# The causal mask of two attentions, added by an accumulating transpose in place of a product

## Chip, core and metric

The kernel runs on one core of a Trainium2 chip. The metric is the device time of one execution in microseconds, as the median of several runs; lower is better.

## The reference

A decoder trunk of two layers over 512 rows of 1024 values, all f32. In each layer a normalised input goes through one projection; four mixers read its columns: a block attention A (4 heads of 64), an RWKV-7 recurrence B, a gated unit C and a differential attention D (4 heads, two maps of 32 each). Their outputs go through one output projection, are added to the input, and a mixture of 32 experts follows (top 1 of 4 groups, top 2 of its 8 experts). What the change touches is the mask of A and D:

```
s = einsum(q, k) * scale
mask = arange(end)[None, :] <= (q0 + arange(128))[:, None]
p = softmax(where(mask, s, -inf))
```

With 512 rows and blocks of 256, attention A is plain causal attention too.

## The kernel before

All engines are programmed by hand and meet at semaphores. In each layer TensorE turns the normalised rows, projects them (L572, L583), and then runs the mixers by one written-out order, `mixer_steps`: steps of the recurrence (P products, T turns, V solve, L levels of the block inverse, Z/B/S chunks, F finish), each followed by some units of attention. Every engine walks the same order, so each has a fixed queue.

An attention unit is one tile of 128 queries (i = 0 to 3) and one head: 16 units for A and 16 for D in each layer. D has two maps in each unit, A one, so there are 48 maps a layer and 96 in all. A map's scores lie in PSUM bank 5 or 6. In `attn(m, u)` TensorE writes the scores of unit u (L754), adds the mask to the last 128 columns (L757), turns the probabilities of unit u-1 (L764, into bank 7) and multiplies those of unit u-2 with the values (L776). VectorE takes the row maximum (L1469) once the mask is in, ScalarE the exponential with its sum (L1138), VectorE the reciprocal and, for D, the difference of the two maps (L1457 to L1462); ScalarE copies the turned probabilities (L1146). The scores of a map wait until the exponential of the map that held the bank is done; L764 waits for the exponential (A) or for L1462 (D).

The constants come in one table, CF: `ident` (identity), `causal` (0 where the key is not after the query, -1e30 elsewhere), `unit` (four 128x128 masks of 0 and 1 for the recurrence; the second is 1 where the partition is not after the column), `head`, `ones` and others. Products with no use for their result (L623, `keep_busy`) stand between some steps of the recurrence that belongs to D.

The recurrence of D needs inverted blocks: VectorE solves them (L1403 to L1406), and SyncE's queue takes them through HBM (L433 to L442) before L663 and L680 read them. The same queue loads the experts' weights in tiles of 2 MB (`fill`, L453 and L455); the first tile is asked for early, the next ones after `mixed_done` (DVE L1494), `mt_ps` and the residual sums (L1587), and the others as tiles come free. A further pass for an expert with over 64 tokens runs only if there is one.

Of the kernel before, what the change touches and what calls it, by code (L numbers as in the profile page):

```python
# [10 lines left out]
ALU = mybir.AluOpType  # L11
# [3 lines left out]
P = 128  # L15
# [22 lines left out]
NEG = -1.0e30  # L38
# [31 lines left out]
def layout(fields):  # L70
    at, out = 0, {}
    for name, n in fields:
        out[name] = (at, n)
        at += n
    return out, at
# [3 lines left out]
CF, NCF = layout([("ident", P), ("causal", P), ("unit", 4 * P), ("head", P), ("ones", P),  # L79
                  ("cosA", NT * 8), ("sinA", NT * 8), ("cosD", NT * 4), ("sinD", NT * 4),  # L80
                  ("down4", GROUPS), ("down8", EPG), ("slot0", NE), ("hop", NE), ("blocks", NOV)])
# [8 lines left out]
def build(nc, x, w_in, w_out, pcol, prow, w2a2, g2, sguT, router, norm2_g, w_gate, w_up, w_down,  # L90
          final_g, cf, cm, out):
    ctx = ExitStack()
    with ctx:
        def sb(name, n, dt=F32):
            return ctx.enter_context(nc.sbuf_tensor(name, [P, n], dt))
# [13 lines left out]
        def at(layer, s, n):  # L109

            return s, layer * adds[s.num] + n
# [13 lines left out]
        CFs = sb("CF", NCF)  # L125
# [13 lines left out]
        PS = [PSALL[:, i * BN:(i + 1) * BN] for i in range(8)]  # L139

        def cst(name):
            lo, n = CF[name]
            return CFs[:, lo:lo + n]
# [236 lines left out]
        for p in range(10):  # L380
            adds[tile_full[p].num] = 16 * (tile_base[p] + sum(at == p for at, _, _ in PLACE))
# [4 lines left out]
        with nc.Block() as block:  # L386
# [155 lines left out]
            def _(pe):  # L542
                mm, tr = nc.tensor.matmul, nc.tensor.transpose
                ident = cst("ident")
                pe.wait_ge(ident_in, 16)

                for layer in range(DEPTH):
# [182 lines left out]
                    def attn(m, u):  # L730
                        s, nm = mix[m], 2 if m == "D" else 1
# [11 lines left out]
                        if u < 16:  # L743
                            i, h = unit_of[u]
                            w = (i + 1) * P
                            for a in range(nm):
                                n = u if m == "A" else 2 * u + a
                                if n >= 2:
                                    pe.wait_ge(*at(layer, s["exped"], n - 1))
                                if m == "A":  # L750
                                    rows = slice((h % 2) * 64, (h % 2) * 64 + 64)
                                else:
                                    rows = slice((h % 2) * 64 + a * 32, (h % 2) * 64 + a * 32 + 32)
                                mm(PS[5 + n % 2][:, 0:w], QKT[rows, h // 2, i * P:w], QKT[rows, 2 + h // 2, 0:w], start=True, stop=False)  # L754
                            for a in range(nm):
                                n = u if m == "A" else 2 * u + a
                                mm(PS[5 + n % 2][:, i * P:w], ident, cst("causal"), start=False, stop=True).then_inc(s["scores"], 1)  # L757
                        if 1 <= u <= 16:
                            i, h = unit_of[u - 1]
                            pe.wait_ge(*at(layer, s["exped"] if m == "A" else s["probs"], u))  # L760
# [5 lines left out]
                        if u >= 2:  # L766
                            n = u - 2
                            i, h = unit_of[n]
# [6 lines left out]
                            for b in range(i + 1):  # L775
                                last = mm(PS[0][:, 0:HD], PT[:, n % 2, b * P:(b + 1) * P], VAD[:, b, v0:v0 + HD],  # L776
                                          start=(b == 0), stop=(b == i))
                            last.then_inc(s["o_ps"], 1)

                    run_mixers(proj=project, rwkv=rwkv, attn=attn, sgu_out=mix_positions)  # L780


# [30 lines left out]
                    for n, ks in ((0, (0, 1, 4, 5)), (0, (2, 3, 6, 7)), (1, range(KD))):  # L813
# [10 lines left out]
                        w = SLOT[n].rearrange("p (k n) -> p k n", k=KD)  # L824
# [170 lines left out]
                    for i in range(NT):  # L995
                        for n in range(2):
                            part = slice(n * CAP, (n + 1) * CAP)
                            mm(PS[2 * i + n][:, :], SHARE_T[part, i * P:(i + 1) * P], YS[0][part, :],
                               start=True, stop=True).then_inc(y2_ps, 1)
# [198 lines left out]
            def _(dve):  # L1198
                V = nc.vector
# [53 lines left out]
                for layer in range(DEPTH):  # L1253
# [19 lines left out]
                    if layer == 0:  # L1273
                        dve.wait_ge(const_in, 33)
                        V.tensor_copy(CMs[:, :], SLOT[5][:, 0:2 * ON_PE * P])
                        ones = CFs[:, CF["ones"][0]:CF["ones"][0] + CAP]
                        V.tensor_tensor_scan(IOTA[:, :], ones, ones, -1.0, ALU.mult, ALU.add)
                        V.tensor_reduce(lane, CFs[:, CF["unit"][0] + P:CF["unit"][0] + 2 * P], AX.X, ALU.add).then_inc(row_named, 1)
                        dve.wait_ge(row_named, 1)
                        V.tensor_scalar(lane, lane, -1.0, float(P), ALU.mult, ALU.add).then_inc(row_named, 1)  # L1280
                        dve.wait_ge(row_named, 2)
                        V.tensor_scalar(upper, lane, float(CAP) - 0.5, None, ALU.is_ge).then_inc(row_named, 1)
                        V.tensor_scalar(TOKEN[:, :, 0], CFs[:, CF["slot0"][0]:CF["slot0"][0] + 2 * NT:2], lane, -NOWHERE, ALU.add, ALU.add)
                        V.tensor_scalar(TAG[:, :, 0], CFs[:, CF["slot0"][0]:CF["slot0"][0] + 16:2], lane, None, ALU.add).then_inc(row_named, 1)
# [294 lines left out]
                    for g in range(8):  # L1579
                        n, i = divmod(g, 4)  # L1580
# [46 lines left out]
                    for half in range(2):  # L1627
                        s = slice(half * HALF, (half + 1) * HALF)
# [156 lines left out]
                    with dve.If(nov > 0):  # L1785
                        with dve.Fori(0, nov) as j:
# [17 lines left out]
                            for r in range(8):  # L1804
                                i, n = divmod(r, 2)
# [206 lines left out]
```

## Time and profile before

| | |
|---|---|
| median of 3 runs | 1883.64 us (1880.81 to 1886.59) |
| profiled execution | 1870.49 us, span 1868.6 us |
| granted TensorE clock, mean | 0.976 |
| TensorE matrix instructions | 1636.9 us busy, x9360 |
| L757, the mask | x192, 40.3 us busy |
| attention units, layer 0 | from 228 to 365 us |
| attention units, layer 1 | from 1150 to 1286 us |

The rows are those of one profiled execution; the span is from its first instruction to its last. Times on the chain of work that ended last count what each step adds to it. The busy time of matrix instructions overlaps from one to the next, since they are pipelined; the distance of their starts is what one costs in a row of them. A granted clock of 1.00 is 2.4 GHz, 0.50 is 1.2 GHz.

### The profile page before, as it was taken

How to read it: one execution, taken by the hardware profiler on the slowest of the kernel's cores; microseconds unless marked ns; L12 is line 12 of the kernel's file. 1: busy time of each engine (PE TensorE's matmuls, PEld its weight loads, DVE VectorE, ACT ScalarE, POOL GpSimd, SP SyncE). 2: the span in 40 equal slices, each digit the busy share in tenths (PEclk: the TensorE clock that was granted, in tenths of full speed). 3: DMA queues.
4: the chain of work that ended last, by engine and by line, in shares of the span. 5: the costliest groups of instructions: out<-in, count | busy, mean ns of one | idle time of the engine just before them, and what ended most of it. 6: DMA issues, size and time to landing. Idle time of an engine off the chain costs nothing.

```text
span 1868.6 us, 22709 instructions
## 1 busy us (share of the span) xinstructions
PE 1636.9 (88%) x9360; PEld 996.0 (53%) x9360; DVE 622.8 (33%) x1419; ACT 278.0 (15%) x638; POOL 158.0 (8%) x175
## 2 busy tenths in 40 slices
PE   7999899999899889777699999899997998888773
PEld 4445567547566555444344456675574665554441
DVE  2174175626212111221322632656251211112115
ACT  3121243401000000000123112332100000000001
POOL 0010000000311111110000101000021111111000
PEclk9999999998999999999999999999998999999997
DMA  9212001056999999999922120011589999999995
GB/s 315 90 45 99 1 4 52 1 247 255 414 424 424 422 425 424 422 423 421 373 75 90 43 96 1 14 41 50 214 362 421 424 424 424 423 424 423 423 421 207
DMA packets 71945, 480.31 MB, mean 257 GB/s; under 512 B 25181, under 2 KB 27165, under 8 KB 37024
## 3 DMA queue, kind: packets, MB, share of 16 engines
q1 hardware_dynamic: 61472, 462.52, 60.2%
q0 software_dynamic: 10368, 16.30, 2.4%
q8 instruction: 77, 1.26, 0.3%
q14 instruction: 28, 0.23, 0.0%
HBM read 468.05 MB, written 28.11 MB: 266 GB/s over the span
## 4 chain that ended last, share of the span: by engine, by line
PE 59%; DMA 27%; DVE 7%; issue 3%; ACT 2%; SPq 1%; POOL 1%; DVEq 0%; POOLq 0%; ACTq 0%
PE banks L583 11%; PE banks L877 11%; PE banks L830 6%; DMA TOK<-in_w_up 6%; PE banks L572 6%; PE banks L892 5%; DMA RING<-in_w_up 5%; DMA RING<-in_w_gate 5%; DMA TOK<-in_w_gate 5%; DMA RING<-in_w_down 2%; PE banks L754 2%; PE banks L855 2%; PE banks L776 1%; PE banks L663 1%; PE banks L757 1%
## 5 line engine op out<-in xcount | busy, mean ns | idle before, releaser
L877 PE MATMUL banks<-RING,XS 128*64 128x256 f32 x2752 | 319.4, 388 | 47.7 <-DMA RING<-in_w_up 28.6
L877 PEld LDWEIGHTS banks<-RING,XS 128*64 128x64 f32 x2752 | 222.4, 140 | 155.3 <-issue 42.8
L583 PE MATMUL banks<-RING,XNT 128*128 128x512 f32 x512 | 224.2, 595 | 0.1
L892 PE MATMUL banks<-RING,XS 128*64 128x512 f32 x768 | 177.4, 602 | 28.3 <-issue 15.2
L1711 DVE SCALAR_TENSOR_TENSOR XS<-banks,TABLE,XS 128x256 f32<-128x256 f32 x58 | 28.1, 484 | 433.3 <-PE banks L877 433.3
L583 PEld LDWEIGHTS banks<-RING,XNT 128*128 128x128 f32 x512 | 96.8, 191 | 117.7 <-issue 116.7
L1177 ACT ACTIVATE XS<-banks,TABLE 128x256 f32<-128x256 f32 x58 | 27.4, 473 | 797.1 <-PE banks L877 797.1
L892 PEld LDWEIGHTS banks<-RING,XS 128*64 128x64 f32 x768 | 60.9, 138 | 112.1 <-issue 112.1
L1753 DVE COPY XS<-banks 128x512 f32<-128x512 f32 x64 | 44.2, 691 | 218.2 <-PE banks L892 191.3
L1923 POOL DMA_INDIRECT y_rows<-XS,SOLVE x64 | 66.2, 1034 | 531.5 <-DVE XS L1753 513.1
L572 PE MATMUL banks<-XNT,RING 128*128 128x512 f32 x256 | 110.2, 592 | 0.0
L877 PE MATMUL banks<-TOK,XS 128*64 128x256 f32 x832 | 94.4, 380 | 14.0 <-DMA TOK<-in_w_gate 7.2
L877 PEld LDWEIGHTS banks<-TOK,XS 128*64 128x64 f32 x832 | 67.9, 137 | 44.0 <-issue 12.7
L830 PE MATMUL banks<-RING,XNT 128*128 128x512 f32 x192 | 86.5, 595 | 1.7 <-ACT XNT L1151 1.7
L572 PEld LDWEIGHTS banks<-XNT,RING 128*128 128x128 f32 x256 | 48.6, 190 | 61.2 <-issue 61.2
L1138 ACT ACTIVATE XNT<-banks,SMALL 128x128 f32<-128x128 f32 (+3 forms) x96 | 50.1, 525 | 129.4 <-DVE SMALL L1469 115.7
L830 PEld LDWEIGHTS banks<-RING,XNT 128*128 128x128 f32 x192 | 35.5, 190 | 42.3 <-issue 40.2
L1469 DVE TENSOR_REDUCE SMALL<-banks 128x1 f32<-128x128 f32 (+3 forms) x96 | 44.5, 488 | 37.7 <-PE banks L757 36.5
L754 PE MATMUL banks<-XNT 32*128 32x128 f32 (+7 forms) x192 | 53.0, 483 | 4.5 <-ACT XNT L1128 2.7
L870 PE MATMUL banks<-CF,XS 128*128 128x128 f32 x256 | 38.7, 296 | 15.9 <-DMA XS<-x_rows,SOLVE 15.9
L1891 POOL DMA_INDIRECT XS<-x_rows,SOLVE x32 | 33.8, 1057 | 190.9 <-PE banks L870 188.6
L883 PE MATMUL banks<-CF,XS 128*128 128x128 f32 x132 | 30.5, 313 | 20.9 <-DVE XS L1711 18.4
(334 smaller groups left out, 1892.2 us busy)
## 6 DMA issues: line engine op xcount, KB each, us to landing
RING<-in_w_down SPq DMA_DIRECT2D x46, 2048.0 KB, 27.1
RING<-in_w_up SPq DMA_DIRECT2D x44, 2048.0 KB, 27.2
RING<-in_w_gate SPq DMA_DIRECT2D x42, 2048.0 KB, 26.3
RING<-in_w_in_blocks SPq DMA_DIRECT2D x12, 2048.0 KB, 9.7
TOK<-in_w_gate SPq DMA_DIRECT2D x12, 2048.0 KB, 32.2
TOK<-in_w_up SPq DMA_DIRECT2D x10, 2048.0 KB, 32.4
XNT<-in_w_down SPq DMA_DIRECT2D x8, 2048.0 KB, 31.1
TOK<-in_w_down SPq DMA_DIRECT2D x6, 2048.0 KB, 24.0
```

The costliest lines, as they stand in the source:

```text
L572: last = mm(bank[:, :], w[:, k, j * P:(j + 1) * P], XNT[:, k, :], start=(k == 0), stop=(k == KD - 1))
L583: last = mm(bank[:, :], XNT[:, k, i * P:(i + 1) * P], w[:, k, :], start=(k == 0), stop=(k == KD - 1))
L754: mm(PS[5 + n % 2][:, 0:w], QKT[rows, h // 2, i * P:w], QKT[rows, 2 + h // 2, 0:w], start=True, stop=False)
L830: last = mm(PS[4 * n + i][:, :], src[:, i * P:(i + 1) * P], w[:, k, :], start=(k == 0), stop=(k == KD - 1))
L855: last = mm(PS[k // 4][:, (k % 4) * P:(k % 4 + 1) * P], X3[:, i, :].rearrange("t (p k) -> t p k", k=KD)[:, :, k], HOT[:, i, :], start=(i = ...
L870: last = tr(PS[k // 4][:, (k % 4) * P:(k % 4) * P + n], rows[:, :, k], ident[0:n, 0:n])
L877: last = mm(bank[f * CAP:(f + 1) * CAP, 0:256], rows[:, k, :], w[:, k, f * 256:(f + 1) * 256], start=(k == 0), stop=(k == KD - 1))
L892: last = mm(PS[5][n * CAP:(n + 1) * CAP, :], HT[:, j, f * CAP:(f + 1) * CAP], w[:, k, n * BN:(n + 1) * BN], start=(k == 0), stop=(k == KF ...
L1138: ac(PB[:, u % 2, a, 0:w], PS[5 + n % 2][:, 0:w], ACT.Exp, bias=nmx[:, col:col + 1], accum_out=sums[:, col:col + 1]).then_inc(s["exped"], 1)
L1469: V.tensor_reduce(nmx[:, base + n:base + n + 1], PS[5 + n % 2][:, 0:w], AX.X, ALU.max, negate=True).then_inc(s["maxed"], 1)
L1753: V.tensor_copy(YS[h], PS[5][:, :]).then_inc(y2_copied, 1)
L1923: pool.indirect_dma_start(y_halves, bass.IndirectOffsetOnAxis(ap=YROW[:, e:e + 1], axis=0), YS[h], None, bounds_check=4 * SEQ - 1, oob_is_ ...
```

## The change

The mask is no longer the moving operand of a product with the identity. Its transpose is the stationary operand of a matrix instruction in transpose mode, with the identity moving, that adds to the bank (`start=False`). The output is (maskT)T, the same mask. For this the `causal` place of CF has to hold the transposed mask; VectorE writes it once, in layer 0, as (unit - 1) * 1e30 from the second mask of `unit`. The mask that comes with CF is overwritten by it and no longer read.

```diff
@@ TensorE, attn(m, u)
                             for a in range(nm):
                                 n = u if m == "A" else 2 * u + a
-                                mm(PS[5 + n % 2][:, i * P:w], ident, cst("causal"), start=False, stop=True).then_inc(s["scores"], 1)
+                                mm(PS[5 + n % 2][:, i * P:w], cst("causal"), ident, start=False, stop=True, is_transpose=True).then_inc(s["scores"], 1)
@@ VectorE, layer 0
                         V.tensor_tensor_scan(IOTA[:, :], ones, ones, -1.0, ALU.mult, ALU.add)
+                        V.tensor_scalar(cst("causal"), CFs[:, CF["unit"][0] + P:CF["unit"][0] + 2 * P], 1.0, -NEG, ALU.subtract, ALU.mult)
                         V.tensor_reduce(lane, CFs[:, CF["unit"][0] + P:CF["unit"][0] + 2 * P], AX.X, ALU.add).then_inc(row_named, 1)
```

## Rows read from the trace of the kernel before

**Rows 1.** The page: busy time by engine, and the chain that ended last.
```profile
PE 1636.9 (88%) x9360; PEld 996.0 (53%) x9360; DVE 622.8 (33%) x1419; ACT 278.0 (15%) x638; POOL 158.0 (8%) x175
...
PE 59%; DMA 27%; DVE 7%; issue 3%; ACT 2%; SPq 1%; POOL 1%; DVEq 0%; POOLq 0%; ACTq 0%
```

**Rows 2.** Windows: us; PE, PEld, DVE, ACT, POOL busy; clock, DMA share, GB/s.
```profile
600.00:900.00 300.00, 248.48 (x1804) 148.80 (x1801) 52.02 (x82) 9.94 (x21) 35.89 (x32) 0.99 1.01 423
```

**Rows 3.** Waits of the DMA queue of SyncE: us in total, times, longest.
```profile
SPq L453 <- DVEq L1494: 174.5, 2, 87.3
...
SPq L492 <- DVE X L1587: 94.8, 8, 21.6
```

**Rows 4.** Instructions of L757 and of L764: duration in ns, min/median/max.
```profile
L757 PE MATMUL banks<-CF x192: 275/275/582, 228.6 to 1274.7; 128*128 128x128 f32 x192
...
L764 PE MATMUL banks<-CF,XNT x160: 272/273/421, 230.1 to 1278.7; 128*128 128x128 f32 x160
```

**Rows 5.** Timeline of TensorE around a pair and a single mask: start, us, what.
```profile
1261.22 0.71 PE L757 MATMUL banks<-CF 128*128 128x128 f32 x4
1261.77 0.49 PE L764 MATMUL banks<-CF,XNT 128*128 128x128 f32 x3
1262.10 0.67 PE L776 MATMUL banks<-TOK,RING 128*128 128x64 f32 x5
...
228.16 0.48 PE L754 MATMUL banks<-XNT 64*128 64x128 f32 x2 [0.69 <-ACT XNT L1128]
228.57 0.49 PE L757 MATMUL banks<-CF 128*128 128x128 f32 x2
```

**Rows 6.** The chain in layer 0: masks, first and last, and two pairs.
```profile
228.64 0.42 PE banks L757 x2
...
290.24 1.15 PE banks L757 x4
...
317.70 0.64 PE banks L757 x4
...
352.49 0.43 PE banks L757 x2
```

**Rows 7.** Windows of layer 0's attention stretches, columns as in rows 2.
```profile
226.00:230.00 4.00, 3.06 (x20) 2.37 (x20) 0.67 (x3) 3.59 (x7) 0.00 (x0) 1.00 0.00 0
...
281.00:285.00 4.00, 3.06 (x26) 2.52 (x26) 0.28 (x1) 2.17 (x4) 0.00 (x0) 1.00 0.18 37
...
288.00:294.00 6.00, 5.77 (x26) 5.14 (x26) 2.24 (x8) 2.27 (x11) 0.00 (x0) 0.50 0.39 92
...
316.00:352.00 36.00, 35.29 (x238) 24.38 (x237) 24.62 (x66) 17.11 (x57) 0.00 (x0) 1.00 0.00 1
```

**Rows 8.** Waits from 225 to 366 us: us in total, times, longest.
```profile
PE banks L764 <- DVE XNT L1462: 2.9, 6, 1.0
PE banks L764 <- ACT RING L1146: 2.8, 4, 1.0
...
DVE SMALL L1469 <- PE banks L757: 18.1, 17, 4.9
```

**Rows 9.** SyncE's queue at the second attention's start, and KB and us to landing.
```profile
287.25 4.09 SPq L442 DMA_DIRECT2D RING<-inv_e  x8
...
RING<-inv_e SPq DMA_DIRECT2D x32, 8.0 KB, 1.7
```

**Rows 10.** The chain behind those blocks, and the same products later.
```profile
291.93 3.16 PE banks L663 x16
295.09 0.89 PE banks L680 x8
...
300.99 1.84 PE banks L663 x16
```

**Rows 11.** Timeline of VectorE where the change adds its instruction.
```profile
24.61 0.26 DVE L1278 TENSOR_REDUCE SMALL<-CF 128x1 f32<-128x128 f32 x1
...
30.45 0.69 DVE L1287 TENSOR_TENSOR RING<-RING,CF 128x512 f32<-128x512 f32 x1 [4.93 <-DMA SMALL<-in_norm_g]
```

## The prediction

> **What bounds the kernel now.** I read the page first: TensorE is busy for 88% of the span and is 59% of the chain that ended last; DMA is 27% of that chain [rows 1]. The windows tell where each rules. From 600 to 900 us (the experts) the 16 DMA engines are full at 423 GB/s and TensorE is busy for 248 of 300 us [rows 2]: time saved on TensorE there would be lost to the weights. The masks are not there. They are 192 instructions of L757, in two stretches of some 137 us, one a layer, where the attention units run between the steps of the RWKV part and DMA is nearly idle. What I must know is whether an earlier end of that stretch reaches the end of the kernel. The waits of the DMA queue answer it: the queue stood 174.5 us in all for DVEq L1494 (mixed_done) and 94.8 us for L1587 (residual sums) [rows 3]. So all expert weights but the first tile are asked for only behind the mixers, and the full DMA stretch keeps its length and only begins earlier. I carry a microsecond saved in the mixers to the end at full value, in each layer.
>
> **What one mask costs, and what its turn will cost.** The mask of a map is one product of 128x128 f32, and the trace has two MATMUL for it, each with its weight load: x192 for 96 maps (275 ns each at the median) [rows 4]. The transpose of L764 is of the same size, is also f32, and has one instruction for each 128x128 (x160 for 160 blocks), of 273 ns. A duration holds the way through the array, so the price is the spacing: four mask instructions start at 1261.22 and the first transpose at 1261.77, which is 0.55 us for five slots (one is the first weight load), and three transposes take 1261.77 to 1262.10, 0.33 us [rows 5]. Both kinds take 0.11 us a slot. The turn thus takes one slot in place of two: 0.11 us saved a map, at the full clock. All 96 maps would give 10.6 us.
>
> **What of it lies on the path.** The chain of layer 0 passes 14 times through a single map (L757 x2) and 8 times through a pair (x4), from 228.64 to 352.49 us [rows 6]; layer 1 has the same counts. That is 14 + 16 = 30 of 48 maps a layer; the other 18 lie beside the L1416 merges, beside the L1387 products, or beside a wait for L1462, and save nothing. 60 x 0.11 = 6.6 us. Three maps of each layer, the pair at 290.24 and the map before it, run at half clock, where a pair takes 1.15 us on the chain against 0.64 [rows 6], so each saves another 0.11: 0.7 us in both layers. The upper bound is 7.3 us.
>
> The lower bound takes only the pairs, where TensorE is busy 35.3 of 36.0 us (316 to 352) [rows 7]: 32 x 0.11 = 3.5 us. The single maps of the first attention share their place with waits for the exponents, and TensorE's own waits in layer 0 are 2.9 us for L1462 and 2.8 us for L1146 [rows 8]; a shorter mask also brings these forward, since the maximum (L1469) waits for it, 18.1 us in 17 cases. So I take three of four parts of the bound and a little: 5.7 us. One cover has to hold: the inverted blocks come by DMA at the start of the second attention. Their last issue ends at 291.34 and lands 1.7 us later, at 293.0 [rows 9], and the first product that reads them (L680) starts at 295.09 [rows 10]. Some 2 us of cover stand against at most 13 maps since 262 us and their half-clock extra, 1.8 us, and the solve moves up itself. No wait should appear.
>
> **The other parts.** The stationary operand is now the mask and the moving one the identity: no instruction more. One VectorE instruction is added, in layer 0 only, which makes the mask on the chip from the `unit` table. The reduction of the same 128x128 at 24.61 takes 0.26 us, and behind this run VectorE idles 4.93 us until L1287 at 30.45 [rows 11]. Price 0 to 0.3 us, I take 0: that wait hides it, and without the cover it would be 0.3 us once. Semaphores and DMAs are as before. The form itself, a transpose that adds to a bank, is not in this trace. Its cost lies between one slot (0.11, as L764) and two (0.22, as the product); it is nearest to L764, so one. There is one more unknown: the first mask starts 0.41 us behind a product of two slots (228.16 to 228.57) [rows 5], so 0.2 us pass when the 64-row operands give way to 128 rows. Both forms have that change, so I count nothing for it.
>
> Sum: 1868.6 - 5.7 = 1862.9 us of span, 1864.8 for the profiled execution (1870.49 before). The median of the runs shown is 13.1 us above that execution; the saving is taken off it: 1883.6 - 5.7 = 1878 us, 0.30% less.
>
> **The rivals.**
> *Nothing gained (the adding form takes two slots, or a wait absorbs each slot).* For it: no row shows the form, and waits for VectorE are close in the pairs. Against it: product to transpose and transpose to product follow at 0.11 us in [rows 5]. Time 1884.
> *The clock, on the other side.* Before, the granted clock fell from 1.00 (2.4 GHz) to 0.50 (1.2 GHz) for 288 to 294 us, after a stretch with idle time on TensorE [rows 7]. What this costs: 16 products of L663 take 3.16 us there and 1.84 later [rows 10], and with L754 and the masks the chain loses some 2.3 us. The change takes work out of just such thin stretches (226 to 230 is busy 3.06 of 4.00 us and still has 1.00). One more fall a layer costs 4.6 us and leaves 1883 (no change). The sign turns at 3 falls more in both layers together, and it is slower by over 0.3% from 5. If the stretch of the pairs (36 us, nearly all TensorE) lost the clock as well, up to 30 us a layer would be added: 1938. Against it: from 281 to 285, where 16 transposes of L740 are most of the work, the clock stayed at 1.00 [rows 7].
> The Trainium skill (TensorE: Matmul & The Clock Gate, PE-mode transpose) says that a transpose doesn't count as busy for the clock as a product does. By that rule the masks would fall out of the activity wholly and the clock rival would be likely; by the row of 281 to 285 they lose half of it at most. The trace speaks against the rule, so I leave that rival small.
> *The mask does not add but overwrites.* Then the change doesn't do what it says: the diagonal blocks hold no scores, the router sees other rows, and an expert with over 64 tokens would bring an overflow pass with three loads of 2 MB, 15 us at 423 GB/s: 1893 or more.
> The Trainium skill (PSUM — Partial Sum Buffer, The four PSUM rules) says that an f32 transpose shares the marks by which a bank adds; no row here shows it.
> *More gained.* If the half-clock fall of each layer went away, another 4.6 us would go: 1873.
>
> **How the numbers follow.** The forecast, 3.5 to 7.3 us, has 0.74; nothing gained 0.12; one or two falls more 0.05; many falls 0.04; overwritten 0.02; more gained 0.03. 0.3% is 5.65 us, about what a measurement here can tell from no change, and it lies on my sum: of the 0.74, 0.42 is beyond it and 0.32 short of it. Faster 0.42 + 0.03 = 0.45; same 0.32 + 0.12 + 0.05 = 0.49, taken as 0.48; slower 0.07. The three runs before spread over 5.8 us, which I add half to either side: from 7.3 saved (1876.3) less 2.8 = 1873.5 to nothing gained (1883.6) and 1.9 of the spread, 1885.5.
>
> **What would show it.** L757 with 96 matrix instructions of about 273 ns and 96 weight loads; a pair on the chain at 0.42 us in place of 0.64; the stretch from the first L754 of a layer to its first L830 shorter by 2 to 3.6 us, and the end of each expert stretch earlier by the same; a clock of 0.50 in one stretch of some 7 us a layer. I am wrong if L757 still takes two slots, if L764 or L680 waits longer by what the masks gave, or if the clock row has more falls.

## The result and the profile after

| | before | after |
|---|---|---|
| median of 5 runs each | 1883.75 us (1880.81 to 1886.59) | 1872.61 us (1868.28 to 1874.56) |
| profiled execution | 1870.49 us, span 1868.6 | 1868.28 us, span 1866.4 |
| granted clock of it, mean | 0.976 | 0.975 |

The ratio is 0.9939 (95% interval 0.9921 to 0.9957): 11.1 us faster. Predicted were 5.7 us and 1878.0; the time lies 0.9 us below the range. Two numbers of this table already disagree: the medians differ by 11.1 us, the two profiled executions by 2.2. The profiled execution after is the fastest of its five; the one before is none of its five and lies 10 us under the lowest of them. Executions that took over 1.5% longer than the others of their kernel (four of 101 of the kernel before, 1909 to 3300 us, and one of a variant, 5798 us) are left out of all figures. The profile says which stretches got shorter, and by how much.

**The instruction.** The instructions of L757 in the trace after (columns as in [rows 4]):

```profile
L757 PEld LDWEIGHTS banks<-CF x96: 137/138/224, 228.1 to 1271.1; 128*128 128x128 f32 x96
L757 PE MATMUL banks<-CF x96: 272/328/474, 228.1 to 1271.2; 128*128 128x128 f32 x96
```

The weight loads of the same line in the trace before:

```profile
L757 PEld LDWEIGHTS banks<-CF x192: 186/189/333, 228.6 to 1274.6; 128*128 128x128 f32 x192
```

There are 96 where [rows 4] have 192, with 96 weight loads. The median of 328 ns in place of 275 is no higher price: the ends of matrix instructions are modelled, so the starts tell the price. The timeline of TensorE after, around the same pair as in [rows 5] and around the first single mask:

```profile
1271.08 0.44 PE L757 MATMUL banks<-CF 128*128 128x128 f32 x2
1271.35 0.60 PE L764 MATMUL banks<-CF,XNT 128*128 128x128 f32 x4
...
227.65 0.48 PE L754 MATMUL banks<-XNT 64*128 64x128 f32 x2 [0.69 <-ACT XNT L1128]
228.06 0.33 PE L757 MATMUL banks<-CF 128*128 128x128 f32 x1
228.23 0.56 PE L701 MATMUL banks<-RING 128*128 128x64 f32 x4
```

The product behind that single mask stood here in the trace before:

```profile
228.90 0.56 PE L701 MATMUL banks<-RING 128*128 128x64 f32 x4
```

From the pair to the transposes behind it pass 0.27 us where 0.55 passed [rows 5], which is 0.14 a map. From the single mask to L701 pass 0.17 us where 0.33 passed (228.57 to 228.90), which is 0.16 a map. Both are more than the slot of 0.11. In a row each form follows at 0.11 us, but the first instruction of a mask holds up the next one longer: by 0.21 us as a product and by 0.165 as a transpose (medians of the distances of starts). The median of the weight load fell as well, from 189 to 138 ns; that it sets this distance is likely, but not shown. By the distances of starts a layer frees 16 x 0.16 for A and 16 x 0.275 for the pairs of D, some 7.0 us at full clock, not the 5.3 of 48 x 0.11. The single mask still starts 0.41 us behind its L754 product, as before.

**The chain.** Layer 0 of the chain that ended last, after: some of the single masks, the pair at half clock with the products behind it, and the first and the last of seven pairs at full clock.

```profile
228.13 0.26 PE banks L757
...
229.20 0.26 PE banks L757
...
231.62 0.26 PE banks L757
...
237.19 0.27 PE banks L757
...
283.93 0.27 PE banks L757
...
288.17 0.62 PE banks L757 x2
...
289.32 3.52 PE banks L663 x16
292.85 1.40 PE banks L680 x8
...
315.97 0.37 PE banks L757 x2
...
349.45 0.37 PE banks L757 x2
```

Against [rows 6]: 0.37 us for a pair where 0.64 stood (predicted 0.42), 0.62 for the half-clock pair where 1.15 stood, 0.26 for a single one where 0.42 stood. Counted over the whole layer, the chain passes 12 single masks and 8 pairs, 28 maps, where it passed 30. Its time in L757 fell from 11.7 to 6.3 us, by 5.4. The stretch got shorter by only 2.7: the other half came back on other steps of the same chain. Steps of VectorE and ScalarE (L1462 and its neighbours, L1138, L1431, L1436) take 2.5 us more of it, L764 and L776 1.8, and L663 and L680 0.9; L754, the row maximum and issue take 2.6 less.

**Who waits.** Waits from 225 to 366 us, after (columns as in [rows 8]; the added VectorE line moves L1462 to L1463 and L1469 to L1470):

```profile
DVE SMALL L1470 <- PE banks L757: 14.6, 14, 4.7
...
PE banks L764 <- DVE XNT L1463: 4.6, 7, 1.1
...
PE banks L764 <- ACT RING L1146: 3.4, 4, 1.2
```

TensorE's two waits were 2.9 and 2.8 us [rows 8]; they are 4.6 and 3.4. So 2.3 us of what was freed in this layer came again as waits. VectorE's wait for the mask fell from 18.1 to 14.6 us.

**The stretch.** The marks that I compare all executions by are the first L740 and the first L830 of a layer, that is from the first transpose of the attention's Q and K to the first product behind the mixers. Timeline of TensorE in layer 0, before:

```profile
225.04 1.04 PE L740 MATMUL banks<-CF,TOK 128*128 128x128 f32 x8
...
367.42 1.13 PE L830 MATMUL banks<-RING,XNT 128*128 128x512 f32 x2 [0.85 <-ACT XNT L1151]
```

The same after, in layer 0 and then in layer 1:

```profile
224.53 1.04 PE L740 MATMUL banks<-CF,TOK 128*128 128x128 f32 x8
...
364.22 4.13 PE L830 MATMUL banks<-RING,XNT 128*128 128x512 f32 x9 [0.84 <-ACT XNT L1151]
...
1146.34 1.04 PE L740 MATMUL banks<-CF,TOK 128*128 128x128 f32 x8
...
1285.91 0.70 PE L830 MATMUL banks<-RING,XNT 128*128 128x512 f32 x1 [0.84 <-ACT XNT L1151]
```

142.38 us became 139.69 in layer 0 and 142.35 became 139.57 in layer 1: 2.69 + 2.78 = 5.5 us. The forecast for both was 5.7.

**The covers and the rest.** Windows after (columns as in [rows 2]), over the places of [rows 7] and [rows 2], each moved with its work:

```profile
225.00:229.00 4.00, 3.06 (x23) 2.33 (x20) 0.47 (x2) 3.55 (x7) 0.00 (x0) 1.00 0.00 0
280.00:284.00 4.00, 3.06 (x26) 2.39 (x26) 0.28 (x1) 2.17 (x4) 0.00 (x0) 1.00 0.18 38
287.00:294.00 7.00, 6.97 (x33) 6.75 (x34) 1.58 (x6) 2.66 (x10) 0.00 (x0) 0.52 0.45 115
315.00:350.00 35.00, 33.52 (x222) 22.08 (x221) 24.47 (x66) 16.35 (x53) 0.00 (x0) 1.00 0.00 1
600.00:900.00 300.00, 244.96 (x1752) 143.51 (x1750) 52.88 (x83) 9.47 (x20) 34.92 (x31) 0.98 1.01 423
```

The clock is as in [rows 7]: 1.00 in the thin stretches and in that of the pairs, one fall to half where the second attention starts. In the pairs' stretch TensorE is busy for 33.5 of 35 us where it was busy for 35.3 of 36 [rows 7]: it has slack now. The experts still fill the DMA engines at 423 GB/s. The added VectorE instruction and the next one on its engine, timeline after:

```profile
24.09 0.20 DVE L1278 TENSOR_SCALAR CF<-CF 128x128 f32<-128x128 f32 x1
...
29.81 0.69 DVE L1288 TENSOR_TENSOR RING<-RING,CF 128x512 f32<-128x512 f32 x1 [4.68 <-DMA SMALL<-in_norm_g]
```

0.20 us, with a wait for DMA of 4.68 us behind it (4.93 before [rows 11]): hidden.

**The way to the end.** The first loads of the expert weights behind the mixers start 3.2 us earlier in layer 0 (0.5 of it was there at the first L740, ahead of every mask), and the loads at the end of that layer's experts 3.8 us earlier. So nothing of the gain is lost in the DMA stretch. Then it shrinks to 0.5 us between 1087 us and the first L740 of layer 1, at 1146.34 (1146.87 before): in this execution the granted clock fell once more at 1119.8 us, for 6.8 us, where the execution before kept 1.00. Nothing that the change touches lies there. Of the 5.5 us gone from the two attention stretches the two profiled spans show 2.2.

### The profile page after: what moved, and what is told of

Same layout as the page of the kernel before. It is cut to its first block, busy times and chain, and to the rows that moved or that the text cites. A ratio compares the mean times of both kernels' runs of the same rounds, so it can differ in the third digit from the quotient of the medians.

```text
span 1866.4 us, 22518 instructions
## 1 busy us (share of the span) xinstructions
PE 1631.3 (87%) x9264; PEld 980.3 (53%) x9264; DVE 622.5 (33%) x1420; ACT 277.8 (15%) x638; POOL 158.7 (9%) x175
## 4 chain that ended last, share of the span: by engine, by line
PE 61%; DMA 23%; DVE 7%; SPq 4%; issue 3%; ACT 2%; another core or an unknown queue 1%; DVEq 0%; POOLq 0%; ACTq 0%
PE banks L877 12%; PE banks L583 12%; PE banks L892 7%; PE banks L830 6%; PE banks L572 6%; DMA TOK<-in_w_up 6%; DMA RING<-in_w_up 5%; DMA RING<-in_w_gate 3%; DMA RING<-in_w_down 2%; DMA TOK<-in_w_gate 2%; SPq L453 2%; DMA SCAN<-in_w_up 2%; PE banks L855 2%; PE banks L754 2%; PE banks L776 1%
## 5 line engine op out<-in xcount | busy, mean ns | idle before, releaser
L877 PE MATMUL banks<-RING,XS 128*64 128x256 f32 x2752 | 318.1, 387 | 53.2 <-DMA RING<-in_w_up 30.0
L877 PEld LDWEIGHTS banks<-RING,XS 128*64 128x64 f32 x2752 | 220.5, 139 | 162.6 <-issue 43.0
L877 PE MATMUL banks<-TOK,XS 128*64 128x256 f32 x832 | 94.4, 380 | 13.9 <-DMA TOK<-in_w_gate 8.1
L877 PEld LDWEIGHTS banks<-TOK,XS 128*64 128x64 f32 x832 | 67.4, 137 | 44.8 <-issue 11.7
L830 PE MATMUL banks<-RING,XNT 128*128 128x512 f32 x192 | 86.5, 595 | 1.7 <-ACT XNT L1151 1.7
L1138 ACT ACTIVATE XNT<-banks,SMALL 128x128 f32<-128x128 f32 (+3 forms) x96 | 50.1, 525 | 123.4 <-DVE SMALL L1470 106.8
L830 PEld LDWEIGHTS banks<-RING,XNT 128*128 128x128 f32 x192 | 35.5, 190 | 42.3 <-issue 40.2
L754 PE MATMUL banks<-XNT 32*128 32x128 f32 (+7 forms) x192 | 53.2, 483 | 5.1 <-ACT XNT L1128 2.7
L883 PE MATMUL banks<-CF,XS 128*128 128x128 f32 x132 | 30.5, 314 | 27.2 <-DVE XS L1712 18.4
L1470 DVE TENSOR_REDUCE SMALL<-banks 128x1 f32<-128x128 f32 (+3 forms) x96 | 44.1, 488 | 30.3 <-PE banks L757 29.4
L1417 DVE COPY_PREDICATED RING<-CM,banks 128x512 f32<-128x512 uint8 x40 | 29.2, 730 | 57.9 <-PE banks L682 30.3
```

What stands on the lines that cost most here:

```text
L830: last = mm(PS[4 * n + i][:, :], src[:, i * P:(i + 1) * P], w[:, k, :], start=(k == 0), stop=(k == KD - 1))
L877: last = mm(bank[f * CAP:(f + 1) * CAP, 0:256], rows[:, k, :], w[:, k, f * 256:(f + 1) * 256], start=(k == 0), stop=(k == KD - 1))
L1138: ac(PB[:, u % 2, a, 0:w], PS[5 + n % 2][:, 0:w], ACT.Exp, bias=nmx[:, col:col + 1], accum_out=sums[:, col:col + 1]).then_inc(s["exped"], 1)
L1470: V.tensor_reduce(nmx[:, base + n:base + n + 1], PS[5 + n % 2][:, 0:w], AX.X, ALU.max, negate=True).then_inc(s["maxed"], 1)
```

## The experiments

All ran in three sets; a set ran on one chip with the kernel before beside it, 10 to 12 executions of each kernel and 31 to 34 of before. Medians of before: 1878.41, 1878.96 and 1879.55 us. The ratio is the recorded one, with its 95% interval; it isn't the quotient of the two medians and differs from it by up to some 0.1%.

| kernel | median us | ratio to before (95%) | layer 0 / layer 1, first L740 to first L830 | mean clock |
|---|---|---|---|---|
| before (first profile) | | | 142.38 / 142.35 | |
| after (first profile) | 1872.61 | 0.9939 (0.9921 to 0.9957) | 139.69 / 139.57 | |
| set 1: before again | 1879.16 | 1.0005 (0.9988 to 1.0022) | 142.35 / 142.34 | 0.9718 |
| set 1: after again | 1875.16 | 0.9981 (0.9963 to 1.0000) | 139.25 / 139.46 | 0.9698 |
| set 1: product, operands swapped | 1876.96 | 0.9994 (0.9978 to 1.0009) | 141.41 / 142.33 | 0.9728 |
| set 1: two turns a mask | 1876.84 | 0.9991 (0.9973 to 1.0010) | 141.39 / 141.40 | 0.9731 |
| set 2: turn in A only | 1880.70 | 1.0005 (0.9984 to 1.0025) | 141.56 / 144.70 | 0.9722 |
| set 2: turn in D only | 1872.51 | 0.9978 (0.9963 to 0.9992) | 140.03 / 141.29 | 0.9758 |
| set 2: turn, falls filled | 1868.93 | 0.9957 (0.9941 to 0.9973) | 139.18 / 137.18 | 0.9777 |
| set 2: product, falls filled | 1872.09 | 0.9972 (0.9957 to 0.9987) | 140.66 / 140.99 | 0.9792 |
| set 3: after, third time | 1874.45 | 0.9971 (0.9955 to 0.9987) | 139.64 / 139.51 | 0.9703 |
| set 3: turn in A only, again | 1879.80 | 1.0002 (0.9978 to 1.0026) | 141.48 / 141.38 | 0.9724 |
| set 3: turn in D only, falls filled | 1869.51 | 0.9955 (0.9941 to 0.9968) | 138.78 / 139.75 | 0.9792 |
| set 3: four turns a mask | 1882.34 | 1.0026 (1.0008 to 1.0044) | 145.11 / 145.23 | 0.9780 |

The mean clock is that over the executions of a kernel; the stretches are those of its one profiled execution.

### Set 1: is it the slot, or the form?

**Before, unchanged**: how far do two runs of the same kernel differ?

> The kernel before, unchanged, against itself, on the chip of the next three. Theory S (slots): the mask turn saves one slot of 0.11 us on the path per map, and the rest of the measured 11 us is another number of falls of the clock, which differ from execution to execution. It expects a ratio within 0.998 to 1.002 here, and a spread of several us in which the runs with a lower mean clock are the longer ones. Theory P (place): the two medians, 1883.75 and 1872.61 us, were taken on different chips or at different times. It expects this kernel near 1872 to 1876 us as well, if the chip is the second one.

Measured 1879.16, ratio 1.0005. The attention stretches are the same to 0.03 us (142.35, 142.34). Yet its profiled span came out longer than the first one, and the windows show where. The kernel before, the execution of the first profile:

```profile
130.00:140.00 10.00, 8.46 (x39) 5.17 (x38) 5.16 (x9) 1.88 (x2) 0.00 (x0) 1.00 0.01 2
200.00:212.00 12.00, 11.62 (x59) 7.53 (x60) 3.10 (x9) 0.79 (x2) 0.00 (x0) 1.00 0.00 1
1120.00:1134.00 14.00, 12.80 (x69) 8.53 (x69) 3.82 (x10) 0.87 (x2) 0.00 (x0) 1.00 0.00 0
```

The same kernel, run again:

```profile
130.00:140.00 10.00, 8.80 (x35) 5.55 (x33) 4.51 (x7) 1.88 (x2) 0.00 (x0) 0.79 0.01 2
200.00:212.00 12.00, 11.18 (x50) 8.00 (x49) 3.53 (x9) 0.28 (x1) 0.00 (x0) 0.72 0.00 1
1120.00:1134.00 14.00, 12.28 (x73) 10.28 (x72) 3.35 (x8) 2.07 (x4) 0.00 (x0) 0.82 0.00 0
```

Three times the granted clock fell to half for 6.8 us where it had stood at 1.00. The first L740 came at 230.5 us in place of 225.0: the two early falls cost 5.5 us. The third cost 3.2. So two executions of one kernel differ by some 9 us, in stretches that differ by falls of the clock and that the change does not touch. As theory S expected, the ratio is within 0.2% of 1; theory P expected 1872 to 1876 us on this chip, which did not come.

**After, unchanged.**

> The changed kernel once more, in rounds with the kernel before. Theory S: 5 to 7 us below the kernel before from slots, up to 11 with the clock: ratio 0.9935 to 0.997. Theory P: ratio 0.9985 to 0.997, 3 to 5 us, as the two profiles showed in the attention stretches.

Measured 1875.16, ratio 0.9981: 3.3 us faster, not 11.1. Theory S had expected 5 to 7 us and missed; the figure is the one of theory P, whose cause (the place, with the kernel before at 1872 to 1876 us) the run before this one does not bear out. The attention stretches lost 3.1 and 2.9 us, as in the first profile: 6.0 in both. The profiled span is 3.3 us shorter than that of before again, so 2.7 are given back, and the trace has the place. From the first product of layer 0's experts (L877) to the first L740 of layer 1 pass 697.6 us here and 695.0 before. One window in the projection of layer 1, before again:

```profile
1055.00:1070.00 15.00, 13.46 (x51) 7.29 (x50) 7.72 (x14) 1.88 (x2) 0.00 (x0) 1.00 0.02 2
```

The same window, after again:

```profile
1055.00:1070.00 15.00, 13.61 (x44) 7.70 (x43) 5.61 (x10) 1.88 (x2) 0.00 (x0) 0.77 0.04 5
```

A fall of 6.8 us, far behind the masks, in work that the change does not touch; TensorE passes 44 instructions in the window where 51 passed.

**The same stationary operand, but as a product** (the turned mask loaded, the identity moving, no transpose mode; as the identity is symmetric the sum is the same):

```diff
-mm(PS[5 + n % 2][:, i * P:w], cst("causal"), ident, start=False, stop=True, is_transpose=True).then_inc(s["scores"], 1)
+mm(PS[5 + n % 2][:, i * P:w], cst("causal"), ident, start=False, stop=True).then_inc(s["scores"], 1)
```

> The changed kernel with a plain product in place of the turn: the mask written on the chip is still the stationary operand and the identity moves, and the transpose mode is off. Two slots a map again; the added VectorE instruction and the exchange of the operands remain. Theory S: all of the gain is the slot, so this is the kernel before within 0.2% (ratio 0.998 to 1.002). A rival (operands): part of the gain comes from what is stationary; then it lies between, at 0.994 to 0.997.

Measured 1876.96, ratio 0.9994, no difference that this tells from before. Its L757:

```profile
L757 PE MATMUL banks<-CF x192: 275/275/582, 233.7 to 1282.2; 128*128 128x128 f32 x192
```

192 instructions again. Exchanging the operands and making the mask on VectorE gain nothing that can be told by themselves, and the distance behind the first instruction (0.21 us) and the weight load (189 ns) are as before; in layer 0 the stretch was 0.9 us shorter because the fall at D's start lasted 3.4 us there, in layer 1 it was 142.33.

**Two turns a mask** (the mask is added twice; a kernel of the turned form with the slots of the product):

```diff
+mm(PS[5 + n % 2][:, i * P:w], cst("causal"), ident, start=False, stop=False, is_transpose=True)
 mm(PS[5 + n % 2][:, i * P:w], cst("causal"), ident, start=False, stop=True, is_transpose=True).then_inc(s["scores"], 1)
```

> The changed kernel with the turn made twice in each map: the mask is added twice, which leaves the masked scores at -2e30 and the others as they are. Two slots a map, both in transpose mode. Theory S: as the kernel before (ratio 0.998 to 1.002), if a transpose counts for the clock as a product does. Theory C (clock): a transpose counts less, so the clock falls more often or elsewhere than with two product slots, or less often: then it differs from the swapped product by more than 0.2%, and the mean clocks differ.

Measured 1876.84, ratio 0.9991: the time of the swapped product within 0.1 us, at the same mean clock (0.9731 and 0.9728). With the slots given back two thirds of the gain in the stretches is gone: they are 141.4 us, 1.0 under before and 1.9 over after. The 1.0 that stays is of the form, not of the count: the first instruction of a mask holds up the next for 0.165 us here too, where it is 0.21 in the swapped product, and by these distances two turns free 1.7 us a layer against two product slots. So the slots carry two thirds of the gain. For the clock no difference between a transpose and a product in its place shows: the means of 12 executions each are 0.0003 apart, with a standard error of 0.001.

### Set 2: which half, and what do the falls hide?

**The turn in A only, the turn in D only** (the other attention keeps two slots; its product reads the turned mask as stationary):

```diff
-start=False, stop=True, is_transpose=True).then_inc(s["scores"], 1)
+start=False, stop=True, is_transpose=(m == "A")).then_inc(s["scores"], 1)
```

and `m == "D"` in the other.

> The changed kernel with the turn for attention A alone; D's maps get the same mask by a product with the mask stationary. Read from the profile: the attention stretch of a layer, from the first turned q and k of A (L740) to the first output product (L830), takes 142.35 us with products and 139.3 to 139.7 with turns. Slots on the path: 11 of A's 16 maps, 1.2 us a layer: a stretch of 141.1 to 141.4 us. A rival (A's maps are hidden behind VectorE): 142.0 or more. The whole time, at the same mean clock, 2 to 2.5 us below the kernel before, which the medians alone can't tell from nothing.

> The changed kernel with the turn for attention D alone. Slots on the path: 19 of D's 32 maps, of which 3 at half clock: 2.1 to 2.4 us a layer, a stretch of 140.0 to 140.3 us, if A's and D's savings add up to the 2.7 to 3.1 of both. A rival (the solve of D's blocks by DMA bounds the start of D): under 1.5 us a layer. The whole time at the same mean clock 3.5 to 4.5 us below the kernel before.

A only: 1880.70, ratio 1.0005, nothing gained. Layer 0's stretch is 0.8 us shorter; layer 1's is 2.4 longer, with a second fall of the clock inside attention A at 1194.5 us. D only: 1872.51, ratio 0.9978; layer 0's stretch is 2.35 us shorter, layer 1's only 1.1, with one more fall at 1148.3. D holds the larger part, as its 32 of 48 maps would have it. In layer 0 the stretch of D only is as expected and that of A only 0.2 us above; in layer 1 both miss, with a fall more. The time of D only is 6.5 us below before by the medians and 4 by the ratio, where 3.5 to 4.5 were expected.

**The falls filled, with the turn and with the product.** Products whose result nothing reads are added on TensorE: in each layer four at D's start, where the clock falls, and two in the last level of the first block inverse (at 195 and 197 us).

```diff
@@ attn(m, u)
                                 if j >= 2:
+                                    if m == "D" and j == 2:
+                                        keep_busy(PS[4], 3 * P)
                                     pe.wait_ge(*at(layer, s["qk_copied"], j - 1))
...
+                            if m == "D":
+                                keep_busy(PS[4], 3 * P)
                             pe.wait_ge(*at(layer, s["qk_copied"], 4))
                         if u < 16:
                             i, h = unit_of[u]
                             w = (i + 1) * P
+                            if m == "D" and u in (1, 2):
+                                keep_busy(PS[4], 3 * P)
@@ the last level of the block inverse, before its wait for de_merged
                                     if n == 3:
+                                        if c == 0:
+                                            keep_busy(PS[7], 3 * P)
                                         pe.wait_ge(*at(layer, s["de_merged"], 8 + q))
```

> The changed kernel with unused products (identity by 384 columns, as L623) in TensorE's waits: 4 at the start of D's attention in each layer, 2 in the last level of the first block inverse. Theory F (falls): the clock falls in these stretches, at the start of D in every execution and near 200 us in some of them, and each fall costs 2 to 5 us. Without them the attention stretch is 2 us shorter (137.5 us), the mean clock of an execution is up by 0.003 to 0.01, and the time is 1868 to 1871 us with a smaller spread: ratio 0.994 to 0.997. Rival: the unused products delay what stands behind them by as much as they give back; then the ratio is that of the changed kernel, 0.998, or above 1.

> The kernel before with the same unused products. With the clock held in both, the change should show by its slots alone: the other kernel of this pair is 5 to 6 us faster than this one (ratio of the two 0.997). Theory F: this kernel is 3 to 6 us faster than the kernel before (0.997 to 0.9985). If the turn had moved the clock, the distance between the two filled kernels would differ from 5.4 us, the difference at equal mean clock in the runs before.

With the turn: 1868.93, ratio 0.9957, the fastest of all kernels here. With the product: 1872.09, ratio 0.9972. The windows of the filled turn at D's start, layer 0 and layer 1:

```profile
284.00:295.00 11.00, 10.65 (x68) 7.69 (x69) 3.49 (x14) 5.33 (x19) 0.00 (x0) 1.00 0.16 25
1203.00:1214.00 11.00, 10.70 (x70) 7.72 (x70) 3.49 (x14) 5.56 (x20) 0.00 (x0) 1.00 0.28 47
```

The fall of [rows 7] is gone in both layers; the one near 200 us is still there (at 202.2 us in this profile), so the two early products did not remove it. Between the two filled kernels lie 3.2 us (standard error 1.1), where 5 to 6 were expected; the filled turn's mean clock is lower by 0.0015. The stretches differ by 1.5 us in layer 0 and 3.8 in layer 1, for in layer 0 the cover of the inverted blocks gives way. The waits from 229 to 369 us of the filled turn hold one that neither before nor after has (L682 is L680, two lines further down):

```profile
PE banks L682 <- DMA RING<-inv_e: 1.8, 1, 1.8
```

With the fall gone TensorE reaches the product before its blocks are back from HBM; with the product form the same wait is 0.5 us. This takes 1.3 us of the turn's gain in layer 0. In layer 1 the filled turn has no such wait (the filled product 0.8) and the shortest stretch of all, 137.18 us, near the 137.5 expected for both layers.

### Set 3: repeats, and the clock by transposes alone

**After a third time, and A only again.** No edit beyond those above.

> The changed kernel a third time. So far it was 11.1 us below the kernel before (5 runs of each) and 3.3 us below it (12 runs against 33). Theory S (slots 5.5 us at equal mean clock, minus what a lower mean clock takes, 0.9 us): ratio 0.9965 to 0.9985, and the first figure was a draw of the falls. Rival: the first figure is the true one; ratio 0.994.

> The turn for attention A alone, again. Its slots save about 1 us a layer in the profile, yet the first time it was 1.4 us above the kernel before in the mean, and its profile had a fall of the clock inside the attention of A that no other profile has. Theory C (the turn makes A's thin stretch thinner and the clock falls more often there): at or above the kernel before once more, 0.9995 to 1.001. Theory S: 1 to 2.5 us below it, ratio 0.9987 to 0.9995.

After: 1874.45, ratio 0.9971. The fall near 1060 us is there again (at 1061.9), and from L877 to the second first L740 pass 698.0 us. A only: 1879.80, ratio 1.0002, with stretches of 141.48 and 141.38, 0.9 us shorter in each layer. But it too has a fall in that place, at 1064.5, and 699.4 us between those marks. So the turn in A shortens what it touches, and in this execution the clock took back more than that further on.

**D only, with the falls filled.** The filled kernel with `is_transpose=(m == "D")`.

> The turn for D alone, with the unused products in TensorE's waits. If A's turn costs clock (theory C), this is the fastest so far: 1865 to 1868 us, below the filled kernel with both turns (1868.9). Theory S: 1869 to 1871, above it, since A's slots are paid again.

Measured 1869.51, ratio 0.9955: as fast as the filled turn in both attentions (1868.93) within the intervals, and where theory S had it. Its wait for the inverted blocks is 0.4 us in layer 0 and 1.4 in layer 1.

**Four turns a mask** (the mask is added four times):

```diff
+for _ in range(3):
+    mm(PS[5 + n % 2][:, i * P:w], cst("causal"), ident, start=False, stop=False, is_transpose=True)
 mm(PS[5 + n % 2][:, i * P:w], cst("causal"), ident, start=False, stop=True, is_transpose=True).then_inc(s["scores"], 1)
```

> The changed kernel with the mask added four times: two slots a map more than the kernel before, 0.22 us each. If every map comes onto the path once the mask is long, 48 x 0.22 = 10.6 us a layer are added to the attention stretch (142.35 to 153); if only the 30 maps of the chain pay, 6.6 us (149). Together with one slot (139.4) and two (142.35) it shows how much of a slot the path pays. The expert stretches stay as they are: the whole time grows by what both stretches grow.

Measured 1882.34, ratio 1.0026. The stretches are 145.11 and 145.23 us: two slots more a map than the product cost 2.8 us a layer net, of the 10.6 that 48 x 0.22 would be. Both expectations, 149 and 153 us, were too high: at D's start a fall of the clock went away, and most of a longer mask is absorbed. In A's part, from the first L740 to D's, no fall stands in these profiles: with one, two and four turns it takes 55.78, 56.39 and 58.5 us. There the second slot costs 0.6 us of 1.75, the next two 2.1 of 3.5. The whole time is 2.8 us over before where the two stretches grew by 5.6, not the same as expected. The added instructions, and those that were there:

```profile
L758 PE MATMUL banks<-CF x288: 272/273/332, 233.5 to 1284.5; 128*128 128x128 f32 x144
...
L759 PE MATMUL banks<-CF x96: 272/273/273, 233.9 to 1284.7; 128*128 128x128 f32 x96
```

Their timeline around a single mask of attention A:

```profile
249.80 0.27 PE L758 MATMUL banks<-CF 128*128 128x128 f32 x1
249.91 0.27 PE L759 MATMUL banks<-CF 128*128 128x128 f32 x1
250.01 0.38 PE L766 MATMUL banks<-CF,XNT 128*128 128x128 f32 x2
```

0.11 us from one to the next, as predicted for the adding form in a row (L766 is L764, two lines further down). The windows at D's start in both layers, first with two turns a mask:

```profile
290.00:305.00 15.00, 13.83 (x84) 11.93 (x84) 6.76 (x19) 4.17 (x17) 0.00 (x0) 0.77 0.45 149
1212.00:1226.00 14.00, 12.17 (x73) 10.37 (x73) 3.82 (x14) 6.21 (x20) 0.00 (x0) 0.76 0.34 91
```

and with four:

```profile
290.00:305.00 15.00, 13.52 (x107) 11.68 (x106) 6.84 (x19) 5.46 (x19) 0.00 (x0) 1.00 0.45 150
...
1212.00:1226.00 14.00, 12.27 (x95) 10.43 (x95) 4.74 (x16) 6.33 (x20) 0.00 (x0) 1.00 0.35 93
```

The fall is gone, though nothing but transposes was added.

### The executions taken together

The kernel before was timed in 97 executions beside the three sets: mean 1878.1 us, 1870.4 to 1885.2, standard deviation 3.4, mean clock 0.9725. The changed kernel in 24: mean 1874.0 us, 1865.0 to 1882.0, deviation 4.1, mean clock 0.9701. The difference is 4.1 us, 0.22%, with a standard error of 0.9 (95%: 2.3 to 5.9). A line through the executions of all kernels gives 0.9 us for 0.001 of mean clock; within one kernel, where nothing but the execution differs, it is 1.2. So the changed kernel's lower clock costs an estimated 2.1 to 2.9 us, and at equal clock it would be 6.2 to 7.0 us faster. By the same two lines the others would stand at: swapped product -0.6 to -0.8 us, two turns 0.0 to -0.2, A only +0.7 to +0.9, D only -1.1 to -2.2, filled turn -3.3 to -5.0, filled product -0.4 to +1.8, four turns +9.2 to +11.1. These are estimates: a fall costs what it does only where TensorE is on the path.

## Why the prediction was right and wrong

**One slot for two: right. 0.11 us a map: too low.** 96 instructions, each 0.11 us behind the one before it in a row. But a mask is mostly not in a row: I took the whole 0.55 us of a pair as slots of 0.11, one of them for the first weight load, and priced the change by the slot alone. The first instruction holds up the next for 0.21 us as a product and 0.165 as a transpose, so a pair saves 0.27 us (predicted 0.22; on the chain 0.37 us are left, predicted 0.42) and a single mask 0.16.

**5.7 us in the two attention stretches: right in the number, by luck.** Measured 5.5, 6.0 and 5.6 us in the three profiles after. Two errors cancel. I counted 30 maps on the chain at 0.11 us, 3.3 us a layer and 0.35 for the half clock; the chain's time in L757 fell by 5.4. And I took off a fifth for waits, where half came back: only 2.7 were gained, TensorE's waits for L1463 and L1146 alone grew by 2.3 us, and it is idle for 16.3 us of layer 0's stretch where it was 13.3. The chain did keep its maps, 28 of 30. Where the time was gained: from the first L740 to D's first L740 the stretch went from 56.82 to 55.78 us, 1.0 for the 11 maps there that I counted at 1.2, and D gave the rest, 1.7 of some 2.4. The other counts go the same way: giving the slot back (two turns) cost 1.9 us a layer of a possible 5.3, and two more on top of that another 3.8 net of the fall that went away, of a possible 10.6. A slot in these stretches is worth a third to a half of itself.

**Carried to the end at full value: right for the DMA stretch; behind it not seen.** The weight loads behind the mixers start 3.2 us earlier and those at the end of the experts 3.8 us earlier in layer 0. But from layer 0's first L877 to layer 1's first L740 pass 691.8 us in the first profile before and 694.4 after, 695.0 and 697.6 in the repeats, 698.0 in the third: 2.6 to 3.0 us longer, in each case with a fall of the clock near 1060 or 1120 us that the execution before did not have. I had priced falls only inside the masks' stretches. Whether the change brings these falls is not shown: the two executions of before differ by 3.2 us between the same marks, and with turns too these marks lie 691.1 to 691.7 us apart in the profiles of D only, of the filled turn and of four turns, none of which has a fall there.

**No wait at the inverted blocks: right.** On the chain L680 starts at 292.85 (295.09 before [rows 10]) with no DMA wait. How near that cover is to its end shows with the fall taken out: the wait is then 0.5 us with the product and 1.8 with the turn in layer 0. L680's first eight took 1.40 us in place of 0.89 [rows 10], since the fall now reaches into them. That is 0.5 us I had not counted.

**VectorE's instruction at nothing: right**, 0.20 us in a wait of 4.68.

**The clock: not by the rule of transposes, but not nothing.** No fall was added in the masks' stretches of the three profiles after, nor was one removed. A fall more in these stretches I priced at 2.3 us; one inside attention A cost 3.1 (58.89 us in place of 55.80 in A only). The Trainium skill (TensorE: Matmul & The Clock Gate, PE-mode transpose) says that a transpose doesn't count as busy for the clock as a product does; by that rule two turns should have run at a lower clock than the swapped product, and four turns should not have lifted a fall. They ran at 0.9731 against 0.9728, and four turns did lift it, at a mean clock of 0.9780: the measurement speaks against the rule here. The rival's other half, that taking work out lowers the clock, is borne out in part: it is 0.9701 against 0.9725, and 0.9777 against 0.9792 with the falls filled, but D only has 0.9758, above before, and no run says why. By the two lines above the lower clock costs the change an estimated 2.1 to 2.9 us of 6.2 to 7.0; the sum had nothing for it. In the profiles the added falls are those between the two attention stretches.

**The mask adds.** The rival "overwrites" did not come: the further pass that it expects is not there, for the two traces differ by the 96 matrix instructions of the mask and no other (9360 and 9264).

**The step that failed** is the last of the sum, "the saving is taken off it": the median of the three runs shown, 1883.6, was taken as the kernel's level, and part of those runs' spread was added on either side (2.8 us below and 1.9 above; half of 5.8 is 2.9). Those three, 1880.8 to 1886.6, lie at the top of what the kernel does: 97 executions have their mean at 1878.1 and reach from 1870.4 to 1885.2. From the mean of 97, 1878.1 - 5.7 would have been 1872.4, against 1872.6 measured. The three are also the first three of the five of the comparison, so that one had before 5.6 us above its mean and after 1.4 us below its own, which with the difference of the means, 4.1, makes the 11.1 us measured. The profiled execution, 13.1 us under the median, was the sign: I noted it and did not follow it. The windows of that execution outside the attention held falls at none of the three places where the repeat had them. The rival "more gained" was not what happened: the fall at D's start stayed.

**Open.** Why the first five and five runs lay so far apart. Medians of five drawn from the two pools differ by 11.1 us or more in about 1.3 of 100 draws. The oddity is on the side of before: a median of 1883.75 or more comes in about 6 of 10000 draws, one of 1872.61 or less for after in 21 of 100. One of the five, 1886.59, lies above all 97. So chance is a thin answer, and nothing here shows a second: neither the chip nor the clock of those five is on record. And what decides where the clock falls outside the mixers. The one near 1060 us stands in two of the three profiles after, in one of two with the turn in A and in the filled one with the turn in D; it stands in neither of before, nor in those of the swapped product, the filled product, D only, the filled turn, two turns and four turns. That is 4 of 10 profiles with a turn and 0 of 4 without, too few to tell, and no run here moved that place alone. It is a possible reason why the turn in A gains nothing in the whole (0.8 us slower, with a standard error of 1.3, over both sets, where its slots gave 0.9 a layer); that is argued, not shown.

## What to carry to other kernels

Price an operation by the distance of starts, not by its duration, and read the distance behind the first instruction of a group apart from that in a row: here 0.21 and 0.165 us against 0.11. Expect that of a saving spread over a chain of handshakes between engines part comes back as waits a few steps on; here it was half. Count a chain in short windows: the list of its longest pieces leaves out just the steps that got short. When the expected change is 0.3%, compare the length of the touched stretch between two marks in the traces, which repeated to 0.5 us in before and in after, ahead of the whole time, which spread over 15 us for one and the same kernel; and where the profiled execution lies far from the median, look for falls of the granted clock before trusting either. Where such a fall stands in the same place each time, a few products of no use ahead of it were worth as much as the slots taken out (0.28% against 0.19 and 0.29%), and then the next cover, here a transfer, is to be looked at.

## What the runs showed of the hardware

- An f32 transpose of 128x128 that adds to a bank is one instruction and follows in a row at 0.11 us, as one that writes it; the f32 product of that size is two, at 0.11 us each. Behind the first instruction of a mask the next starts after 0.21 us with the product and 0.165 with the transpose; the medians of their weight loads are 189 and 138 ns.
- Falls of the granted clock from 1.00 to 0.50, for 3.4, 6.8 or 10.2 us each, come and go between executions of the same kernel outside the stretches with the masks: three of 6.8 us were 8.7 us. The one at D's start was in every profile of before and after, in both layers, and went away in the filled kernels and with four turns.
- Over the executions of all kernels 0.001 of mean granted clock was worth 0.9 us of some 1875, within one kernel 1.2.
